# A two-layer encoder on one core: query tiles and later U tiles as one matmul of 512 columns and one of 256, with the halves added on DVE

## Chip, core and metric

The kernel runs on one core of one Trainium2 chip. The time is that of one execution on the device, in microseconds. The engines are TensorE (PE; PEld is its loading of weights), VectorE (DVE), ScalarE (ACT), GpSimd (POOL) and SyncE (SP), which only issues the loads of weights here.

## What is computed

256 tokens of width 1024 pass through two layers. Each has a token mixer (gated DeltaNet in layer 0, Mamba-2 SSD in layer 1) and then a PEER mixer, which retrieves experts by product keys. All is in float32. The change is in PEER:

```python
def _peer(h, w_q, sub_keys, u_tab, v_tab):
    q = (ht @ w_q).reshape(n_tok, PEER_HEADS, 2, PEER_HALF)
    s = jnp.einsum('thpd,hpkd->thpk', q, sub_keys).astype(jnp.float32)
    s_top, i_top = lax.top_k(s, PEER_TOPK)
    ...
    best, pos = lax.top_k(cand, PEER_TOPK)
    expert = jnp.take_along_axis(cand_id, pos, axis=-1)
    gate = jax.nn.softmax(best, axis=-1)
    ...
        act = jax.nn.gelu(jnp.einsum('thkd,td->thk', u_tab[eb], xb).astype(jnp.float32), approximate=False) * gb
        return jnp.einsum('thk,thkd->td', act.astype(v_tab.dtype), v_tab[eb])
```

There are 128 x 128 experts, 8 heads, two keys a head and the 16 best of each.

## The kernel before

**Split operands.** A float32 product is made of three faster ones. Each operand is split into a high part, rounded to the type fp32r, and a low part, the rest; the kernel computes high x high, high x low and low x high. `part_mm` issues the three matmuls. The tokens' parts are `hT[0]` and `hT[1]`, each 8 slices of 128 x 256 (slice k covers 128 of the 1024 channels). A weight tile of 128 x 1024 (512 KB) is loaded by SP into one of four places of `ring`. ScalarE copies it, half by half, into the high part (`split_half`), and POOL or DVE subtracts to get the low part (`rest_of_unit`). `w_part` has room for four halves, that is two tiles, so half s of tile n+2 can be converted once TensorE has used half s of tile n.

**The dense PEER.** The kernel doesn't gather experts. It goes through all 128 tiles of U (128 experts each) and computes the hidden value of every expert for every token: tile i gives 128 experts x 256 tokens in bank `PS[i % 2]` (`hidden`, which calls `columns`: 8 slices, 24 matmuls of 256 columns). Meanwhile it builds `p_map`, the gate of each expert for each token, mostly zeros. The weighted hidden values then multiply the 128 tiles of V (`values`). A PEER layer runs in these stages:

1. Query: 16 tiles of `peer_wq`, banks 4 and 5 in turn (`route` on TensorE). ScalarE copies each finished bank to `p_qT`. Then come the scores, and DVE's top-16 and gates, which take until about tile 56 of U.
2. Early U tiles, 0 to 55: ScalarE's Gelu writes straight into `p_map`.
3. Late rounds, tiles 56 to 119. In round q of these TensorE runs `hidden` of tile 57+q, then the map matmuls of four tokens (`maps4`). DVE runs `weigh_maps` (L1291: the last round's maps, out of their bank, times what stands in `p_map`), `one_hots` for the next round (L1281 and L1284) and `weigh_hidden` (L1299: the Gelu of tile 56+q times its row of the map). ScalarE runs `late` (L1645: the Gelu of tile 56+q into `p_act`, between the two halves of the high part of tile 58+q, L1376) and `weighed_rows` for the next round (L1666 and L1672). POOL makes both low halves of each tile (L1735).
4. Tiles 120 to 127, without maps.
5. Value stage: DVE splits each row of the map (`parts`, L1333 and L1334) and makes the low parts of the V tiles from the third on (L890); TensorE runs 12 matmuls of 512 columns a tile.

Every engine runs its own list in order, and the lists meet in counting semaphores: `lo_ready` and `half_used` for the halves of weights, `p_gelu` for a Gelu (TensorE waits for that of tile i-2 before it writes the bank again), `p_gated` for the product of a row, `p_mapps` for maps in their bank.

## Time and profile before

| | |
|---|---|
| median of 3 runs | 2286.61 us (2285.64 to 2288.24) |
| profiled execution | 2287.4 us |
| its span, first to last instruction | 2285.2 us |
| TensorE, mean granted clock | 0.974 |
| query stage, layer 0 | about 293 to 338 us |
| late rounds, layer 0 | about 508 to 746 us |
| value stage, layer 0 | from 783 us |

The profile is of one execution. An engine's busy time is that of its instructions from start to end, and matmuls overlap, so a busy TensorE says that it is never empty, not how fast it goes; the pace is read from the starts of neighbouring instructions. The clock is given as a share of 2.4 GHz. Layer 1 has the same PEER stages with nearly the same windows (late rounds from 1651 us).

### The profile page before, as it was taken

The page shows a single profiled execution, that of the slowest core. Times are in us where ns is not written, and L with a number is a line of the kernel's source. Part 1 is how long each engine was busy: PE and PEld are TensorE (multiplying, and loading weights), DVE is VectorE, ACT ScalarE, POOL GpSimd, SP SyncE. Part 2 cuts the span into 40 slices and gives each one's busy share as a digit, 9 for nine tenths or more (in the row PEclk, how much of TensorE's full clock was granted, in tenths as well). Part 3 has the DMA queues.
Part 4 walks back from the last instruction along what each step waited for, and adds up shares of the span by engine and source line. Part 5 has one row for each costly group of instructions (what it writes and reads, how often), then busy time and mean ns, then how long its engine had stood idle before and what let it go on. Part 6 is the DMA issues. An engine that isn't in the chain of part 4 may idle for free.

```text
span 2285.2 us, 46234 instructions
## 1 busy us (share of the span) xinstructions
PE 2172.6 (95%) x14320; PEld 1976.9 (87%) x14320; DVE 1547.2 (68%) x3465; ACT 1332.4 (58%) x2706; POOL 1112.2 (49%) x883
## 2 busy tenths in 40 slices
PE   7989799999999999999898878999999999999998
PEld 6969699999999988888797557999999999888886
DVE  4776319985666577777767882199856665777776
ACT  6744355577777544444565664555777775444444
POOL 6851378987666600000176566779876775000000
PEclk9989899999999999999999888999999999999999
DMA  5510254555444566665544114545544445666664
GB/s 166 167 56 1 65 166 148 172 168 154 140 138 138 171 193 193 192 194 191 174 139 127 58 65 132 170 148 169 173 149 141 141 138 165 194 193 193 193 193 147
DMA packets 93891, 343.72 MB, mean 150 GB/s; under 512 B 10688, under 2 KB 10752, under 8 KB 93168
## 3 DMA queue, kind: packets, MB, share of 16 engines
q1 hardware_dynamic: 92592, 338.21, 47.2%
q0 software_dynamic: 928, 4.10, 0.6%
q8 instruction: 47, 0.77, 0.1%
q10 hardware_dynamic: 288, 0.34, 0.0%
q14 instruction: 36, 0.29, 0.0%
HBM read 341.56 MB, written 1.05 MB: 150 GB/s over the span
## 4 chain that ended last, share of the span: by engine, by line
PE 77%; POOL 7%; DVE 7%; issue 5%; ACT 3%; DMA 0%; POOLq 0%; DVEq 0%; ACTq 0%
PE bank L358 75%; POOL w_lo L1735 7%; DVE arena L1155 2%; DVE arena L1143 1%; DVE w_lo L890 1%; ACT w_hi L1376 1%; PE bank L378 0%; PE bank L521 0%; DMA small<-in_ssd_d 0%; ACT arena L1402 0%; ACT arena L1376 0%; DVE arena L863 0%; DVE arena L967 0%; DVE arena L988 0%; DVE arena L1198 0%
## 5 line engine op out<-in xcount | busy, mean ns | idle before, releaser
L1735 POOL TENSOR_TENSOR w_lo<-ring,w_hi 128x512 fp32r<-128x512 f32 x744 | 994.9, 1351 | 684.6 <-ACT w_hi L1376 672.3
L1376 ACT ACTIVATE w_hi<-ring 128x512 fp32r<-128x512 f32 x1280 | 801.9, 628 | 520.6 <-PE bank L358 518.9
L358 PE MATMUL bank<-hT_hi,w_hi 128*128 128x256 f32 x2688 | 780.5, 290 | 8.3 <-POOL w_lo L1735 6.3
L358 PE MATMUL bank<-hT_lo,w_hi 128*128 128x256 f32 x2688 | 761.7, 283 | 0.0
L358 PE MATMUL bank<-hT_hi,w_lo 128*128 128x256 f32 x2688 | 761.6, 283 | 0.0
L358 PEld LDWEIGHTS bank<-hT_hi,w_hi 128*128 128x128 f32 x2688 | 516.6, 192 | 19.3 <-POOL w_lo L1735 18.8
L358 PEld LDWEIGHTS bank<-hT_lo,w_hi 128*128 128x128 f32 x2688 | 517.0, 192 | 0.0
L358 PEld LDWEIGHTS bank<-hT_hi,w_lo 128*128 128x128 f32 x2688 | 516.1, 192 | 0.0
L890 DVE TENSOR_TENSOR w_lo<-ring,w_hi 128x512 fp32r<-128x512 f32 x536 | 377.2, 704 | 172.8 <-ACT w_hi L1376 167.6
L358 PE MATMUL bank<-w_hi,p_ag_hi 128*128 128x512 f32 x1024 | 398.4, 389 | 0.0
L358 PE MATMUL bank<-w_lo,p_ag_hi 128*128 128x512 f32 x1024 | 398.4, 389 | 0.0
L358 PE MATMUL bank<-w_hi,p_ag_lo 128*128 128x512 f32 x1024 | 398.3, 389 | 0.0
L358 PEld LDWEIGHTS bank<-w_lo,p_ag_hi 128*128 128x128 f32 x1024 | 192.2, 188 | 40.1
L358 PEld LDWEIGHTS bank<-w_hi,p_ag_lo 128*128 128x128 f32 x1024 | 192.2, 188 | 39.9
L358 PEld LDWEIGHTS bank<-w_hi,p_ag_hi 128*128 128x128 f32 x1024 | 192.2, 188 | 39.6
L1291 DVE TENSOR_TENSOR arena<-bank,arena 128x512 f32 (+1 forms) x128 | 88.6, 692 | 166.6 <-PE bank L358 166.6
L358 PEld LDWEIGHTS bank<-arena 128*128 128x128 f32 x1072 | 136.1, 204 | 36.8 <-POOL arena L1811 13.2
L358 PE MATMUL bank<-arena 128*128 128x128 f32 (+2 forms) x1072 | 147.6, 294 | 17.6 <-POOL arena L1811 7.1
L908 DVE SCALAR_TENSOR_TENSOR arena<-bank,small,arena 128x254 f32<-128x254 f32 x192 | 92.6, 483 | 55.9 <-ACT arena L1376 50.7
L1672 ACT ACTIVATE work<-work,small 128x128 f32<-128x128 f32 x256 | 112.7, 488 | 20.2 <-ACT work L1666 19.6
L1334 DVE TENSOR_TENSOR p_ag_lo<-arena,p_ag_hi 128x256 fp32r<-128x256 f32 x256 | 111.0, 434 | 8.9
L1645 ACT ACTIVATE work<-bank 128x256 f32<-128x256 f32 x144 | 55.1, 383 | 84.0 <-PE bank L358 84.0
(236 smaller groups left out, 2329.6 us busy)
## 6 DMA issues: line engine op xcount, KB each, us to landing
ring<-in_peer_u SPq DMA_DIRECT2D x256, 512.0 KB, 3.5
ring<-in_peer_v SPq DMA_DIRECT2D x256, 512.0 KB, 3.5
ring<-in_peer_wq SPq DMA_DIRECT2D x32, 512.0 KB, 3.5
ring<-in_gdn_qkv SPq DMA_DIRECT2D x24, 512.0 KB, 3.5
ring<-in_ssd_xbc SPq DMA_DIRECT2D x24, 512.0 KB, 3.5
ring<-in_ssd_z SPq DMA_DIRECT2D x16, 512.0 KB, 3.5
ring<-in_ssd_out SPq DMA_DIRECT2D x16, 512.0 KB, 3.5
ring<-in_gdn_z SPq DMA_DIRECT2D x8, 512.0 KB, 3.5
```

Source lines behind the costliest of these rows:

```text
L358: return pe.matmul(o, w, r, start=first, stop=last)
L890: dve.tensor_tensor(w_part[1][:, s, :], ring[:, n % RING, hf * 512:(hf + 1) * 512], w_part[0][:, s, :].bitcast(F32), ALU.subtract).then_in ...
L908: ins = dve.scalar_tensor_tensor(o, bank[:, lo + s:hi + s], taps[:, m, j:j + 1], o, ALU.mult, ALU.add)
L1143: last = dve.tensor_scalar(s_E[:, h % 2, st, d, :], PS[h % 2][:, d * T + st * P:d * T + (st + 1) * P], s_ac[:, st, d * SH + h:d * SH + h + ...
L1155: last = dve.scalar_tensor_tensor(s_M[:, h % 2, st, d, :], s_CB[:, g, st, d, :], s_dt[:, st, d * SH + h:d * SH + h + 1], s_E[:, h % 2, st, ...
L1291: dve.tensor_tensor(v, PS[2 + q % 4][:, :].rearrange("p (t i) -> p i t", t=4), v, ALU.mult).then_inc(SEM["p_mul"], 1)
L1334: dve.tensor_tensor(p_ag[1][:, i % 2, :], v, p_ag[0][:, i % 2, :].bitcast(F32), ALU.subtract).then_inc(SEM["p_ag"], 1)
L1376: return act.activation(o, i, ACT.Copy, scale=scale)
L1645: act.activation(p_act[:, i % 2, :], PS[i % 2][:, 0:T], ACT.Gelu).then_inc(SEM["p_gelu"], 1)
L1672: act.activation(row, row, ACT.Relu, bias=p_T[:, 2, tok], scale=p_minus[:, tok]).then_inc(SEM["p_hotS"], 1)
L1735: pool.tensor_tensor(w_part[1][:, s, :], ring[:, n % RING, hf * 512:(hf + 1) * 512], w_part[0][:, s, :].bitcast(F32), ALU.subtract).then_i ...
```

## The change

The two parts of the tokens now lie in one tensor, `hT_both`, so that one matmul can stream both. `columns_wide` does for a tile what `columns` does: with the high weights loaded it streams 512 columns, the 256 high and the 256 low ones, into the two halves of a bank, and with the low weights it adds 256 high columns to the second half. Each tile's bank now holds two halves whose sum is the result. It is used for the query tiles and for U tiles 56 to 127. The early U tiles keep `columns`.

DVE adds the halves with a `tensor_reduce`: in the query stage straight into `p_qT` (ScalarE's copy goes away), in the late rounds into a new tile `p_raw` (`add_halves`), from which ScalarE's Gelu reads. So ScalarE waits for a new semaphore, `p_halves`, instead of for TensorE's `half_used`. On DVE `add_halves` of a tile stands last in the round, and `weigh_hidden` is of the tile before. The last 8 rows are weighed ahead of the first two `parts` of the value stage; before, they stood behind them. Loads and other matmuls don't change.

```diff
@@ -145,7 +145,8 @@
         x_sb = sb("x_sb", [P, NT, D])
 
 
-        hT = [sb("hT_" + s, [P, KD, T], F32R) for s in ("hi", "lo")]
+        hT_both = sb("hT", [P, 2, KD, T], F32R)
+        hT = [hT_both[:, p, :, :] for p in range(2)]
         ring = sb("ring", [P, RING, D])
         w_part = [sb("w_" + s, [P, SPLIT, D // 2], F32R) for s in ("hi", "lo")]
         p_ag = [sb("p_ag_" + s, [P, 2, T], F32R) for s in ("hi", "lo")]
@@ -282,6 +283,7 @@
 
 
         row = [flat(p[0:SH, :, :], "s t") for p in p_ag]
+        p_raw = sb("p_raw", [P, T])[:, :]
         pick = sb("pick", [SH, SH], F32R)[:, :]
 
 
@@ -404,6 +406,18 @@
                         await_h(fresh, k)
                         last = part_mm(o, lambda p: w_part[p][:, s, kk * P:(kk + 1) * P],
                                        lambda p: hT[p][:, k, :], k == 0, k == KD - 1)
+                    last.then_inc(half_used, 1)
+
+            def columns_wide(bank, n, it=0, step=0, fresh=None):
+
+                for hf in range(2):
+                    s = half(n, hf, it, step)
+                    for kk in range(KD // 2):
+                        k = KD // 2 * hf + kk
+                        await_h(fresh, k)
+                        c = slice(kk * P, (kk + 1) * P)
+                        mm(bank[:, :].rearrange("p (e t) -> p e t", e=2), w_part[0][:, s, c], hT_both[:, :, k, :], k == 0, False)
+                        last = mm(bank[:, T:2 * T], w_part[1][:, s, c], hT[0][:, k, :], False, k == KD - 1)
                     last.then_inc(half_used, 1)
 
             def rows_of(n, src, first, last_one, it=0, step=0):
@@ -728,7 +742,7 @@
                     if m >= 2:
                         pe.wait_ge(SEM["p_q"], HP * lyr + m - 1)
 
-                    by_channel(("pq", lyr, m), 4 + m % 2, None if m else 2 * lyr + 1)
+                    columns_wide(PS[4 + m % 2], at[("pq", lyr, m)], fresh=None if m else 2 * lyr + 1)
                 pe.wait_ge(SEM["p_q"], HP * (lyr + 1))
                 pe.wait_ge(keys_loaded, 16 * (lyr + 1))
                 for g in range(8):
@@ -745,7 +759,10 @@
                 if tiles or i >= 2:
 
                     pe.wait_ge(SEM["p_gelu"], it * tiles + (P * lyr + i - 1))
-                columns(PS[i % 2][:, 0:T], n, it, 8)
+                if i < EARLY:
+                    columns(PS[i % 2][:, 0:T], n, it, 8)
+                else:
+                    columns_wide(PS[i % 2], n, it, 8)
 
             def values(lyr, i, n, it=0, tiles=0, first=False, last_one=False):
                 pe.wait_ge(SEM["p_ag"], it * tiles + (P * lyr + i + 1))
@@ -1215,6 +1232,9 @@
                 return all_four(lambda v, top, idx: dve.max_index(idx[:, 8:16], top[:, 8:16], v))
 
             def route(lyr):
+                for m in range(HP):
+                    dve.wait_ge(half_used, 2 * (at[("pq", lyr, m)] + 1))
+                    dve.tensor_reduce(p_qT[:, m, :], PS[4 + m % 2][:, :].rearrange("p (e t) -> p t e", e=2), AX.X, ALU.add).then_inc(SEM["p_q"], 1)
                 for g in range(8):
                     t, first_head = g // 2 % 2, 8 * (g // 4) + 4 * (g % 2)
                     dve.wait_ge(SEM["p_s"], 8 * lyr + g + 1)
@@ -1299,16 +1319,24 @@
                     dve.tensor_tensor(row, p_act[:, i % 2, :], row, ALU.mult).then_inc(SEM["p_gated"], 1)
                     dve.wait_ge(SEM["p_gated"], it * 4 + ((P - EARLY) * lyr + i - EARLY + 1))
 
+                def add_halves(i, it=0):
+
+                    dve.wait_ge(half_used, it * 8 + 2 * (tables[lyr] + i + 1))
+                    if not isinstance(it, int) or i > EARLY:
+                        dve.wait_ge(SEM["p_gelu"], it * 4 + (P * lyr + i))
+                    b = PS[i % 2]
+                    dve.tensor_reduce(p_raw, b[:, :].rearrange("p (e t) -> p t e", e=2), AX.X, ALU.add).then_inc(SEM["p_halves"], 1)
+
                 def maps_and_hidden(it, first=False, last=False):
                     for q in range(4):
+                        i, loop = (EARLY + 4 * it + q, 0) if isinstance(it, int) else (EARLY + q, it)
                         if not first or q:
                             weigh_maps(it, q - 1)
                         if not last or q < 3:
                             one_hots(it, q + 1, first)
-                        if isinstance(it, int):
-                            weigh_hidden(EARLY + 4 * it + q)
-                        else:
-                            weigh_hidden(EARLY + q, it)
+                        if not first or q:
+                            weigh_hidden(i - 1, loop)
+                        add_halves(i, loop)
 
                 one_hots(0, 0, True)
                 maps_and_hidden(0, True)
@@ -1316,6 +1344,10 @@
                     maps_and_hidden(it)
                 maps_and_hidden(T // 16 - 1, last=True)
                 weigh_maps(T // 16, -1)
+                for i in range(EARLY + T // 4, P):
+                    add_halves(i)
+                    weigh_hidden(i - 1)
+                weigh_hidden(P - 1)
 
             def experts(lyr):
                 n0 = tables[lyr]
@@ -1337,9 +1369,6 @@
                 dve.wait_ge(SEM["p_mul"], 64 * (lyr + 1))
                 parts(0)
                 parts(1)
-                for i in range(EARLY + T // 4, P):
-                    dve.wait_ge(SEM["p_gelu"], P * lyr + i + 1)
-                    dve.tensor_tensor(p_map[:, i, :], p_act[:, i % 2, :], p_map[:, i, :], ALU.mult).then_inc(SEM["p_gated"], 1)
                 dve.wait_ge(SEM["p_gated"], (P - EARLY) * (lyr + 1))
                 dve.wait_ge(lo_ready, 2 * (n1 + 2))
                 with dve.Fori(0, P // 4 - 1) as it:
@@ -1614,10 +1643,7 @@
 
             def route(lyr):
                 for m in range(HP):
-                    split_half(at[("pq", lyr, m)] + 2, 0)
-                    act.wait_ge(half_used, 2 * (at[("pq", lyr, m)] + 1))
-                    copy(p_qT[:, m, :], PS[4 + m % 2][:, 0:T]).then_inc(SEM["p_q"], 1)
-                    split_half(at[("pq", lyr, m)] + 2, 1)
+                    split(at[("pq", lyr, m)] + 2)
                 for g in range(8):
                     t, first_head = g // 2 % 2, 8 * (g // 4) + 4 * (g % 2)
                     act.wait_ge(SEM["p_sps"], 8 * lyr + g + 1)
@@ -1638,11 +1664,11 @@
                 def late(i, it=0):
 
                     split_half(n0 + i + 2, 0, it, 8)
-                    act.wait_ge(half_used, it * 8 + 2 * (n0 + i + 1))
+                    act.wait_ge(SEM["p_halves"], it * 4 + ((P - EARLY) * lyr + i - EARLY + 1))
                     if not isinstance(it, int) or i >= EARLY + 2:
 
                         act.wait_ge(SEM["p_gated"], it * 4 + ((P - EARLY) * lyr + i - EARLY - 1))
-                    act.activation(p_act[:, i % 2, :], PS[i % 2][:, 0:T], ACT.Gelu).then_inc(SEM["p_gelu"], 1)
+                    act.activation(p_act[:, i % 2, :], p_raw, ACT.Gelu).then_inc(SEM["p_gelu"], 1)
                     split_half(n0 + i + 2, 1, it, 8)
 
                 for i in range(4):
```

## Rows read from the trace of the kernel before

**Rows 1.** The page, section 1: busy time and share of the span.

```profile
PE 2172.6 (95%) x14320; PEld 1976.9 (87%) x14320; DVE 1547.2 (68%) x3465; ACT 1332.4 (58%) x2706; POOL 1112.2 (49%) x883
```

**Rows 2.** Windows of layer 0: busy us of PE, PEld, DVE, ACT, POOL; clock.

```profile
293.00:337.70 44.70, 44.70 (x370) 44.70 (x370) 1.71 (x5) 23.82 (x47) 36.97 (x29) 0.99 0.55 167
427.00:464.00 37.00, 36.13 (x278) 33.70 (x277) 36.90 (x29) 21.18 (x38) 35.07 (x23) 1.00 0.53 164
508.00:746.00 238.00, 238.00 (x2022) 238.00 (x2021) 141.96 (x300) 190.41 (x441) 169.76 (x130) 1.00 0.46 144
...
800.00:900.00 100.00, 100.00 (x443) 82.81 (x442) 74.33 (x148) 46.35 (x74) 0.00 (x0) 1.00 0.64 193
```

**Rows 3.** The chain of waits over the late rounds, 508 to 746 us.

```profile
507.96 238.07 PE bank L358 x2020
```

**Rows 4.** Timeline of TensorE, one late round.

```profile
563.08 0.36 PE L358 MATMUL bank<-hT_hi,w_hi 128*128 128x256 f32 x1
563.28 0.28 PE L358 MATMUL bank<-hT_lo,w_hi 128*128 128x256 f32 x1
563.40 0.28 PE L358 MATMUL bank<-hT_hi,w_lo 128*128 128x256 f32 x1
...
566.84 0.36 PE L358 MATMUL bank<-hT_hi,w_hi 128*128 128x256 f32 x1
```

**Rows 5.** Timeline of DVE, a late round and one four later.

```profile
563.51 0.69 DVE L1291 TENSOR_TENSOR arena<-bank,arena 128x512 f32 x1 [1.26 <-PE bank L358]
564.36 0.69 DVE L1281 TENSOR_TENSOR p_ag_hi<-bank,work 128x512 fp32r<-128x512 f32 x1
...
565.60 0.42 DVE L1299 TENSOR_TENSOR arena<-work,arena 128x256 f32 x1
...
578.58 0.69 DVE L1291 TENSOR_TENSOR arena<-bank,arena 128x512 f32 x1 [1.26 <-PE bank L358]
```

**Rows 6.** Timeline of ScalarE, the same round.

```profile
562.55 0.38 ACT L1645 ACTIVATE work<-bank 128x256 f32<-128x256 f32 x1 [0.58 <-PE bank L358]
562.83 0.62 ACT L1376 ACTIVATE w_hi<-ring 128x512 fp32r<-128x512 f32 x1
...
564.34 0.88 ACT L1672 ACTIVATE work<-work,small 128x128 f32<-128x128 f32 x2 [0.17 <-ACT work L1666]
565.12 0.62 ACT L1376 ACTIVATE w_hi<-ring 128x512 fp32r<-128x512 f32 x1
...
566.61 0.62 ACT L1376 ACTIVATE w_hi<-ring 128x512 fp32r<-128x512 f32 x1
```

**Rows 7.** Timeline of POOL, the next round.

```profile
567.31 1.29 POOL L1735 TENSOR_TENSOR w_lo<-ring,w_hi 128x512 fp32r<-128x512 f32 x1 [0.15 <-ACT w_hi L1376]
```

**Rows 8.** DVE's tensor_reduce, by line: duration ns min/median/max.

```profile
L1258 DVE TENSOR_REDUCE arena<-arena x32: 673/676/686, 450.7 to 1628.4; 128x32 f32<-128x512 f32 x32
```

**Rows 9.** Timeline in gated DeltaNet: ScalarE released by DVE.

```profile
147.94 0.42 DVE L979 TENSOR_TENSOR arena<-arena 128x256 f32<-128x256 f32 x1
...
148.40 0.42 ACT L1494 ACTIVATE arena<-arena 128x256 f32<-128x256 f32 x1 [1.60 <-DVE arena L979]
```

**Rows 10.** Timeline, early tiles beside the top-16: TensorE released by POOL.

```profile
436.43 3.44 POOL L1735 TENSOR_TENSOR w_lo<-ring,w_hi 128x512 fp32r<-128x512 f32 x2
...
439.92 0.19 PEld L358 LDWEIGHTS bank<-hT_hi,w_hi 128*128 128x128 f32 x1 [0.21 <-POOL w_lo L1735]
...
440.15 0.28 PE L358 MATMUL bank<-hT_lo,w_hi 128*128 128x256 f32 x1
```

**Rows 11.** Timelines of TensorE, ScalarE and DVE where the value stage begins.

```profile
782.94 0.40 PE L358 MATMUL bank<-w_hi,p_ag_hi 128*128 128x512 f32 x1
...
783.14 0.39 ACT L1645 ACTIVATE work<-bank 128x256 f32<-128x256 f32 x1 [0.75 <-PE bank L358]
...
787.16 0.28 DVE L1333 CAST p_ag_hi<-arena 128x256 fp32r x1
787.48 0.42 DVE L1334 TENSOR_TENSOR p_ag_lo<-arena,p_ag_hi 128x256 fp32r<-128x256 f32 x1
```

More of the change, by code:

```diff
@@ L306, in hybrid_encoder @@
             "s_cbps s_cb s_bc s_d s_e s_off s_m s_yps s_y s_ss s_mean s_root "
-            "p_q p_sps p_s p_ex p_exd p_key p_Tps p_Tsb p_hot p_hotS p_hotB p_dist p_mapps p_mul p_gelu p_gated p_ag_hi p_ag "
+            "p_q p_sps p_s p_ex p_exd p_key p_Tps p_Tsb p_hot p_hotS p_hotB p_dist p_halves p_mapps p_mul p_gelu p_gated p_ag_hi p_ag "
             "finished stored").split()}
```

## The prediction

> **What bounds the kernel now.** I read the page first: TensorE is busy 95% of the span and no other engine above 68% [rows 1]. A share over the span doesn't say what ends a stage, so I took windows of one layer. In the query stage, in the late rounds and in the value stage TensorE is busy in all of each window at a granted clock of 0.99 to 1.00, its upper level of 2.4 GHz [rows 2]. The chain of waits over the late rounds is one unbroken piece of matmuls, 238 us long [rows 3]. So in the stages that the change touches the pace is TensorE's, and time is gained by shortening its queue, as long as nobody else then becomes late. That needs the timeline of each engine over one round. The reader is to see in it that a late round takes 3.77 us (15.07 us for four) [rows 5], that DVE works 2.51 us of it and then waits for TensorE, and that ScalarE's Gelu starts 0.53 us before TensorE opens the next tile at 563.08 [rows 4, 6].
>
> Matmuls of 256 columns follow each other at 0.120 us [rows 4], those of 512 at 0.226 us (100 us for 443) [rows 2]. A U tile of 24 matmuls takes 2.88 us, which leaves 0.89 us of a late round for its map matmuls.
>
> **The change, part by part: TensorE.** For each of a tile's 8 slices of the contraction three matmuls of 256 columns (0.360 us) become one of 512 and one of 256 (0.346 us): 0.014 us less a slice, 0.11 us a tile. The columns streamed are the same, and only one matmul's fixed part goes. The tile falls to 2.77 us, a half of it to 1.38 us, the late round to 3.66 us. Touched are 16 query tiles and 72 late U tiles in each of two layers, 1408 slices: 19.7 us if nothing else moved. What the 256-column matmul costs directly behind one of 512 no row shows. Its columns alone bound it at 0.107 us (256 at 2.4 GHz) from below and 0.120 us is its row; I take the row, since the 512-column stream also runs 0.013 us over its columns.
>
> The rows show 0.013 us over the column time at both sizes. The Trainium skill (TensorE: Matmul & The Clock Gate, Back-to-back issue gap) gives N/2.4 + 2.5 ns, so three matmuls would take 328 ns and two 325 ns, and all 1408 slices would give back 3.5 us instead of 19.7 us. I go by the rows.
>
> **ScalarE and DVE in the query stage.** The copy of the finished bank (0.38 us) goes from ScalarE to DVE, as a reduce over the two halves. DVE is busy 1.71 us in this stage [rows 2] and takes it within the 2.77 us of the next tile. The nearest row for it reads 512 elements a partition and takes 0.676 us [rows 8]; DVE's other work on 512 columns of a bank takes 0.69 us [rows 5], and I take 0.69 us. POOL needs 1.27 us a half, 2.55 us a tile (36.97 us for 29) [rows 2], under 2.77 us. So the stage gains 32 x 0.11 = 3.5 us. Only the last bank of each layer is seen in full, because the scores wait for it: 0.69 - 0.38 = 0.3 us, 0.6 us in all. Net -2.9 us.
>
> **The late rounds.** Here the Gelu of tile i no longer waits for TensorE alone. It waits for DVE's sum, and DVE issues that sum last in its round: behind the map product, the one-hots and the product of the tile before (weigh_maps, one_hots, weigh_hidden). The first of these waits for maps that TensorE runs after tile i. Behind the Gelu on ScalarE stands the second half of tile i+2's high part, behind that POOL's low part, and TensorE needs both in the middle of tile i+2. I lay this out from T, TensorE's first U matmul after the maps (563.08) [rows 4]:
>
> - the map product starts 0.43 us after T, and the tile product ends 2.51 us later (563.51 to 566.02) [rows 5];
> - 0.16 us for DVE to see its own signal, as between the first two rows of its round [rows 5]; then the sum, 0.69 us;
> - 0.04 us to ScalarE [rows 9], 0.28 us from the start of the Gelu to that of the high part, 0.62 us for it [rows 6];
> - 0.08 us to POOL (567.23 to 567.31), 1.29 us for the low part [rows 7], 0.05 us to TensorE (439.87 to 439.92), and 0.11 us because a matmul after a wait is followed at 0.23 us instead of 0.12 us [rows 10].
>
> That is 6.26 us after T. TensorE is then in the round after the next T, and has half a tile (1.38 us) and the maps (0.89 us) left before the following one. Two rounds take 6.26 + 1.38 + 0.89 = 8.53 us, one takes 4.27 us, where TensorE alone would need 3.66 us and takes 3.77 us now. So TensorE stands about 0.6 us in each tile, and a round is 0.50 us longer. In the kernel before the same ring has ample room: the Gelu starts before T, the second high part ends 0.37 us after it, and POOL is done long before TensorE comes there.
>
> The other waits fit inside 4.27 us. ScalarE's rows for the next maps end at T + 6.5 (Gelu start at 3.83, 2.67 us from there to the end of its row at 564.34) [rows 6] and are wanted at T + 7.6. The first half of tile i+3 is ready at T + 8.5, when TensorE comes for it, and a little lateness there is hidden by the stall in the middle. The bank is released at T + 4.3, which is hidden in the same way. DVE ends its round at T + 3.8 and is idle until the next maps. SP's loads are for tiles further on.
>
> There are 64 such rounds a layer. I take 63, one to close the ring: 126 x 0.50 = +63 us. The 7 tiles after them have no maps. There DVE is free when the tile ends, and the low part comes about 3.3 us after it, before the 4.15 us (a tile and a half) at which it is wanted. They gain 14 x 0.11 = 1.6 us.
>
> **The start of the value stage.** Now TensorE goes from the last U tile to the first V tile at once (782.94), and the last Gelu follows 0.20 us later [rows 11], since DVE had already split the first two rows of the map. In the changed kernel both splits stand behind the last product. So TensorE waits for: 0.20 us, the sum 0.69, 0.04, the Gelu 0.38, 0.04, the product 0.42 [rows 5], 0.16, the cast and the rest 0.28 + 0.04 + 0.42 [rows 11], 0.05. That is 2.7 us a layer, +5.4 us. The two V tiles that follow (12 x 0.226 = 2.7 us each) cover DVE's start on the third.
>
> **The sum.** +63 - 1.6 + 5.4 - 2.9 = +63.9 us on the profiled execution's 2287.4 us, 2351.3 us. The median of the runs is 0.8 us lower: 2350.5 us.
>
> **Bounds.** Chain, short: the 512-column successor at 0.107 us (-0.05 us in a half) and all four handoffs and the restart at nothing (-0.44 us) give 8.04 us for two rounds, 4.02 us each, +32 us. Chain, long: POOL's half beside a busy DVE took 1.72 us (3.44 us for two) [rows 10] instead of 1.29 us, and DVE will be busier; two rounds of 8.96 us, 4.48 us each, +27 us on the forecast, 2378 us.
>
> **Rivals.** *The ring stays open.* The second half of tile i+2 is ready in time and TensorE keeps the pace: -19.7 + 5.4 + 0.6 = -13.7 us, 2273 us, faster. For it speaks that ScalarE and POOL have idle time in each round now. It decides if the low part comes by T + 5.05 (2 x 3.66 - 1.38 - 0.89), 1.2 us earlier than my sum; the queue order leaves no step out. Chance 0.10. *Only the bank binds.* The halves come in time, but tile i+2 can't start before Gelu i has ended (T + 4.26): two rounds of 4.26 + 0.11 + 2.77 + 0.89 = 8.03 us, 4.01 us each, 126 x 0.24 + 0.9 = +31 us, 2318 us. Chance 0.08. *POOL or the sum is slower than its row*, as in the long bound, 2378 us: 0.15. *The clock falls.* With TensorE standing one part in seven, and 2.7 us once a layer, its clock could drop to 1.2 GHz for stretches. A tile's 6144 columns then take 5.12 us, a round with doubled maps 6.9 us, and 20 such rounds bring 2403 us. Against it: with a wait in each half tile, beside the top-16, it kept 1.00 [rows 2]. Chance 0.03. *The parts cancel* within the bound below: 0.02. The forecast itself: 0.62.
>
> **How the numbers follow.** The range of 2317 to 2380 us runs from the bank's case to the long bound and leaves out the open ring and the clock. A measurement of this kernel can tell about 0.2%, 4.6 us, from no change. Faster holds the open ring and a little more, 0.11; the same 0.03; slower 0.86.
>
> **What the profile after would show.** Late rounds 4.2 to 4.4 us apart at DVE's map product, with TensorE stopped once in the middle of a tile, by POOL; Gelu starting some 3.8 us after T instead of before it; 0.346 us for each pair of matmuls; query tiles 2.77 us apart; a gap of about 2.7 us before the first V matmul. Rounds of 3.66 us would refute the ring, rounds of 4.0 us with the stop at a tile's start would show the bank, and a POOL half or a DVE sum much over 1.3 or 0.7 us the long case.

## The result, and the profile after

The kernel became slower: 2402.2 us median of 4 runs (2394.25 to 2405.38) against 2286.97 us (2285.64 to 2288.24), a ratio of 1.0499 (95% interval 1.0486 to 1.0512). The forecast was 2350.5 us with a range of 2317 to 2380 us. The direction was right and the size was not: the loss is 115 us, 1.8 times the 64 us forecast.

The profiled execution of after took 2394.25 us, the shortest of its four; its span is 2392.4 us. The two spans, cut at DVE's map products and at TensorE's matmuls, show where the 107.3 us between them went:

| stretch, us | before | after | difference |
|---|---|---|---|
| start to the first late map product, layer 0 | 525.76 | 521.16 | -4.60 |
| 63 late rounds, layer 0 | 237.30 | 288.21 | +50.91 |
| last map product to the last U matmul | 19.76 | 19.19 | -0.57 |
| from there to the first late map product, layer 1 | 886.43 | 889.98 | +3.55 |
| 63 late rounds, layer 1 | 237.30 | 289.21 | +51.91 |
| last map product to the last U matmul | 19.76 | 19.19 | -0.57 |
| from there to the end | 358.86 | 365.50 | +6.64 |

The first and the fourth stretch also hold mixers, where the clock differs between executions (the last section has it). So nearly all of it lies in the late rounds, 102.8 us in both layers: a round takes 4.58 us instead of 3.77 us. The page, section 1, answers to [rows 1]:

```profile
PE 2189.7 (92%) x12912; PEld 1902.8 (80%) x12912; DVE 1717.2 (72%) x3641; ACT 1317.2 (55%) x2674; POOL 1109.6 (46%) x883
```

DVE is up by 170 us, of which the 144 sums of the late tiles are 100 us. TensorE is still "busy" 92%, and nothing on the line tells of a loss of 5%. The windows do. These are the query stage, late rounds, and the value stage later on (against [rows 2]):

```profile
293.00:337.70 44.70, 43.92 (x260) 38.72 (x259) 11.31 (x18) 20.27 (x32) 41.20 (x32) 1.00 0.54 177
520.00:760.00 240.00, 206.76 (x1259) 176.19 (x1258) 180.20 (x312) 152.11 (x364) 133.70 (x105) 1.00 0.36 113
...
900.00:1000.00 100.00, 100.00 (x443) 82.81 (x442) 73.85 (x147) 46.55 (x74) 0.00 (x0) 1.00 0.61 194
```

In the late rounds TensorE is empty for 33 us of 240 at the full clock, and the chain of waits over 520 to 740 us, which was one piece of matmuls before [rows 3], has none of them in it:

```profile
by line: POOL w_lo L1761 49.6%; issue 49.6%; POOLq L1759 1.2%; POOLq L1771 0.4%
```

The timelines of one pair of rounds say why, TensorE first (against [rows 4]), with the weight load that waited in the middle of the tile:

```profile
566.00 0.47 PE L360 MATMUL bank<-hT,w_hi 128*128 128x512 f32 x1
...
568.86 1.05 PE L360 MATMUL bank<-work,p_ag_lo 128*128 128x128 f32 x8
571.05 0.49 PE L360 MATMUL bank<-hT,w_hi 128*128 128x512 f32 x1 [1.13 <-ACT work L1671]
...
572.86 0.19 PEld L360 LDWEIGHTS bank<-hT,w_hi 128*128 128x128 f32 x1 [0.47 <-POOL w_lo L1761]
...
574.39 1.05 PE L360 MATMUL bank<-work,p_ag_hi 128*128 128x128 f32 x8
575.19 0.47 PE L360 MATMUL bank<-hT,w_hi 128*128 128x512 f32 x1
```

Then DVE, ScalarE and POOL in the same round (against [rows 5 to 7]):

```profile
566.37 0.69 DVE L1311 TENSOR_TENSOR arena<-bank,arena 128x512 f32 x1 [1.59 <-PE bank L360]
567.22 0.69 DVE L1301 TENSOR_TENSOR p_ag_hi<-bank,work 128x512 fp32r<-128x512 f32 x1
567.82 0.72 DVE L1304 TENSOR_SCALAR work<-bank,work 128x128 f32<-128x128 f32 x2
568.46 1.12 DVE L1319 TENSOR_TENSOR arena<-work,arena 128x256 f32 x1
569.77 0.69 DVE L1328 TENSOR_REDUCE p_raw<-bank 128x256 f32<-128x512 f32 x1 [0.19 <-DVE arena L1319]
```

```profile
570.50 0.42 ACT L1671 ACTIVATE work<-p_raw 128x256 f32<-128x256 f32 x1 [2.57 <-DVE p_raw L1328]
570.82 0.62 ACT L1405 ACTIVATE w_hi<-ring 128x512 fp32r<-128x512 f32 x1
```

```profile
568.01 1.29 POOL L1761 TENSOR_TENSOR w_lo<-ring,w_hi 128x512 fp32r<-128x512 f32 x1 [0.88 <-ACT w_hi L1405]
571.51 1.29 POOL L1761 TENSOR_TENSOR w_lo<-ring,w_hi 128x512 fp32r<-128x512 f32 x1 [2.22 <-ACT w_hi L1405]
```

From T = 566.00 to the next such point, 575.19, are 9.19 us for two rounds (the mean of the layer is 9.15 us). This is the forecast's ring, link by link: map product, one-hots, the product of a row (L1319), the sum, the Gelu, the second high half, POOL's low half, TensorE at 572.86, half a tile and the maps. One link has another size. The product of the row was put at 0.42 us and took 1.12 us. It starts at 568.46 and ends at 569.58; POOL's half runs from 568.01 to 569.30. Of the 63 products of layer 0's late rounds 59 start while POOL is at a half, and each of these ends 0.28 to 0.29 us after that half. The sum takes its forecast 0.69 us and POOL its 1.29 us. Over all rounds (durations min/median/max by source line):

```profile
L1319 DVE TENSOR_TENSOR arena<-work,arena x144: 415/723/1537, 523.1 to 2029.5; 128x256 f32 x112, 128x256 f32<-128x256 f32 x32
...
L1328 DVE TENSOR_REDUCE p_raw<-bank x144: 691/692/693, 517.5 to 2027.3; 128x256 f32<-128x512 f32 x144
```

Where the value stage begins (against [rows 11]), TensorE's last U matmul starts at 828.56 and the first V matmul at 833.37, 4.81 us later, where before there were 0.12 us:

```profile
828.56 0.28 PE L360 MATMUL bank<-hT,w_lo 128*128 128x256 f32 x1
833.37 0.51 PE L360 MATMUL bank<-w_hi,p_ag_hi 128*128 128x512 f32 x1 [4.53 <-issue]
...
834.10 0.63 PE L360 MATMUL bank<-w_hi,p_ag_lo 128*128 128x512 f32 x1
834.53 0.63 PE L360 MATMUL bank<-w_hi,p_ag_hi 128*128 128x512 f32 x1
```

```profile
829.54 2.94 DVE L1319 TENSOR_TENSOR arena<-work,arena 128x256 f32<-128x256 f32 x2
```

```profile
834.00:838.00 4.00, 4.00 (x12) 3.06 (x12) 0.69 (x1) 0.65 (x2) 0.00 (x0) 0.62 0.49 175
838.00:842.00 4.00, 4.00 (x19) 3.32 (x18) 2.65 (x6) 1.88 (x3) 0.00 (x0) 1.00 0.38 99
```

Two products take 2.94 us there beside POOL's last three halves, and eight V matmuls then follow the one before at 0.43 us instead of 0.23 us: the granted clock of 834 to 838 us is 0.62, mostly the lower level, 1.2 GHz. In the 50 us from the last U matmul on, 192 V matmuls start, where before 220 did; 28 x 0.227 us = 6.4 us a layer, and the last line of the table has 6.64 us.

### The profile page after: what moved, and what is told of

Its sections match the earlier page's. It is cut to its first block, busy times and chain, and to the rows that moved or that the text cites. A ratio compares the mean times of both kernels' runs of the same rounds, so it can differ in the third digit from the quotient of the medians.

```text
span 2392.4 us, 43818 instructions
## 1 busy us (share of the span) xinstructions
PE 2189.7 (92%) x12912; PEld 1902.8 (80%) x12912; DVE 1717.2 (72%) x3641; ACT 1317.2 (55%) x2674; POOL 1109.6 (46%) x883
## 3 DMA queue, kind: packets, MB, share of 16 engines
HBM read 341.56 MB, written 1.05 MB: 143 GB/s over the span
## 4 chain that ended last, share of the span: by engine, by line
PE 49%; POOL 21%; issue 20%; DVE 7%; ACT 3%; POOLq 1%; DMA 1%; DVEq 0%; ACTq 0%
PE bank L360 48%; POOL w_lo L1761 21%; DVE arena L1172 2%; DVE arena L1160 1%; DVE w_lo L907 1%; PE bank L535 1%; ACT w_hi L1405 0%; PE bank L380 0%; DMA small<-in_ssd_d 0%; POOLq L1759 0%; ACT arena L1405 0%; ACT arena L1431 0%; DVE arena L880 0%; DVE arena L984 0%; DVE arena L1005 0%
## 5 line engine op out<-in xcount | busy, mean ns | idle before, releaser
L360 PE MATMUL bank<-hT,w_hi 128*128 128x256 f32 (+1 forms) x3968 | 993.5, 330 | 88.1 <-ACT work L1671 70.1
L360 PEld LDWEIGHTS bank<-hT,w_hi 128*128 128x128 f32 x3968 | 665.0, 191 | 183.8 <-issue 81.5
L360 PE MATMUL bank<-hT,w_lo 128*128 128x256 f32 x2688 | 756.7, 282 | 0.0
L360 PEld LDWEIGHTS bank<-hT,w_lo 128*128 128x128 f32 x2688 | 512.8, 191 | 0.0
L1671 ACT ACTIVATE work<-p_raw 128x256 f32<-128x256 f32 x144 | 60.4, 419 | 211.7 <-DVE p_raw L1328 211.7
L360 PE MATMUL bank<-w_hi,hT 128*128 128x512 f32 x384 | 135.9, 417 | 13.5 <-ACT arena L1598 10.0
L1328 DVE TENSOR_REDUCE p_raw<-bank 128x256 f32<-128x512 f32 x144 | 99.6, 692 | 66.9 <-PE bank L360 44.6
L1319 DVE TENSOR_TENSOR arena<-work,arena 128x256 f32 (+1 forms) x144 | 123.7, 859 | 0.1
```

Of the source, the lines that this page charges most:

```text
L360: return pe.matmul(o, w, r, start=first, stop=last)
L1319: dve.tensor_tensor(row, p_act[:, i % 2, :], row, ALU.mult).then_inc(SEM["p_gated"], 1)
L1328: dve.tensor_reduce(p_raw, b[:, :].rearrange("p (e t) -> p t e", e=2), AX.X, ALU.add).then_inc(SEM["p_halves"], 1)
L1671: act.activation(p_act[:, i % 2, :], p_raw, ACT.Gelu).then_inc(SEM["p_gelu"], 1)
```

## Experiments

All ratios are against the kernel before on the same chip. "Rounds" are the mean distance of the 64 late map products of layer 0. The theory after the result was: the ring holds, and what made it longer is the product of a row, held up by POOL when both read SBUF. The rivals: the ring is longer for some other wait; the wide matmuls are slow themselves; the clock.

**The query stage alone.** U tiles and the order of DVE as before.

> Only the query tiles use the 512-column matmul and DVE's sum; the U tiles, their Gelu and the order of DVE's late rounds are those of the kernel before. My theory, by which the added time all comes from the late rounds and the start of the value stage: 32 tiles at 2.77 us instead of 2.88 us, less 0.6 us for the longer last copies, so 2.9 us less than before, about 2284 us. Rival, that part of the loss comes from DVE working beside POOL already in the query stage: slower than before, 2290 us or more.

Measured: 2282.33 us (11 runs), ratio 0.9982 (0.9973 to 0.9991), -4.0 us. The query tiles of after stand 2.77 us apart (`hT,w_hi` at 293.10, 295.87, 298.64). This part gains what was forecast, -2.9 us, or a little more.

**The wide matmuls without the sum.** Query and U tiles 56 to 127 as in after, but nobody adds the halves: ScalarE reads the first half of the bank as before, so the low weights' and low tokens' share is left out.

> All matmuls of the change, but nothing adds the halves: ScalarE reads the first half of the bank, in the query stage and for each Gelu, as it read the bank before, and DVE's rounds are those of before. The part of each product that lies in the second half (low tokens and low weights) is left out of the result. It prices the matmuls alone. By the rows of before (0.120 and 0.226 us) 1408 slices give back 0.014 us each: 19.7 us less than before, 2267 us, late rounds of 3.66 us. By N/2.4 + 2.5 ns of the Trainium skill only 3.5 us less, 2283.5 us. Rival to both, that a 256-column matmul behind a 512-column one costs more than 0.120 us: no gain, 2287 us.

Measured: 2269.97 us (2268.0 to 2273.69), ratio 0.9933 (0.9918 to 0.9948), -16.4 us. Rounds are 3.684 us, 0.08 us less than before where 0.11 us had been forecast, and the chain over 560 to 740 us is matmuls alone again. TensorE's timeline:

```profile
600.53 0.39 PE L360 MATMUL bank<-hT,w_hi 128*128 128x512 f32 x1
600.76 0.27 PE L360 MATMUL bank<-hT,w_lo 128*128 128x256 f32 x1
600.87 0.40 PE L360 MATMUL bank<-hT,w_hi 128*128 128x512 f32 x1
```

A pair takes 0.345 us (four take 1.38 us from 599.84 to 601.22), as forecast. The matmuls do save some 16 us, so the loss comes with the sum, its place and the order behind it. The formula of the Trainium skill (TensorE: Matmul & The Clock Gate, Back-to-back issue gap), which the page gives for an isolated matmul and by which 3.5 us would have come back, does not hold for these streams: the pair's 345 ns are 25 ns over the 320 ns of its 768 columns at 2.4 GHz, 12.5 ns for each matmul and not 2.5.

**The Gelu's output in PSUM.** In the late rounds ScalarE writes it to a free bank, so `weigh_hidden` reads one operand from PSUM and one from SBUF. Nothing else moves.

```diff
+        def acted(i, rounds=True):
+            return PS[6][:, (i % 2) * T:(i % 2 + 1) * T] if rounds else p_act[:, i % 2, :]
...
-                    act.activation(p_act[:, i % 2, :], p_raw, ACT.Gelu).then_inc(SEM["p_gelu"], 1)
+                    act.activation(acted(i, not isinstance(it, int) or i < EARLY + T // 4), p_raw, ACT.Gelu).then_inc(SEM["p_gelu"], 1)
```

> The changed kernel, with one thing different: in the late rounds the Gelu writes to PSUM bank 6 instead of to SBUF, so that DVE's product of the hidden row (0.42 us in the kernel before, 0.90 us on average in the changed one) has only one operand in SBUF. My theory now: the ring through DVE, ScalarE and POOL sets the round, and it is 0.7 us longer in two rounds than I added up because this product and POOL's low half, both with two operands in SBUF, slow DVE down when they meet. Then the product falls to about 0.42 us, two rounds take 8.5 us instead of 9.2 us, and the time falls by 126 x 0.34 = 43 us to about 2359 us. Rival, that the product is long because DVE is waiting inside it for something else or that the ring is not what binds: product or round unchanged, 2400 us.

Measured: 2355.09 us (2354.26 to 2360.85), ratio 1.0299 (1.0283 to 1.0315). Groups of instructions over 560 to 740 us, first of after, then of this kernel:

```profile
L1319 DVE TENSOR_TENSOR arena<-work,arena 128x256 f32 x40 | 35.1, 877 | 0.0
```

```profile
L1322 DVE TENSOR_TENSOR arena<-bank,arena 128x256 f32 x42 | 17.4, 413 | 0.0
```

The product is back at 0.413 us every time, POOL working as before beside it. Rounds are 4.235 us, where the ring with a product of 0.42 us had been forecast at 4.27 us. This is the experiment that settles the mis-sized term: 47 us of the loss hang on where one operand lies. TensorE still waits at the start of every second tile, for the Gelu that frees the bank, and again in its middle for POOL:

```profile
641.57 0.49 PE L363 MATMUL bank<-hT,w_hi 128*128 128x512 f32 x1 [0.42 <-ACT bank L1674]
```

**The sum first in its round,** ahead of the map product, instead of last.

```diff
                     for q in range(4):
+                        add_halves(i, loop)
                         if not first or q:
                             weigh_maps(it, q - 1)
...
                             weigh_hidden(i - 1, loop)
-                        add_halves(i, loop)
```

> The changed kernel with DVE's sum of the halves first in its round, ahead of the map product, the one-hots and the product of the row before, instead of last. All work is the same. My theory: the loss comes from the sum's place in DVE's queue, which closes a ring of two rounds. With the sum first the Gelu follows the tile's end by about 1 us, the low part is ready 3.3 us after the tile, over a microsecond early, and the ring is open. The round is then the larger of TensorE's 3.66 us and DVE's own work (3.2 us, waits of 0.3 us, and up to 0.8 us where it meets POOL): 3.7 to 4.0 us, so 2275 to 2320 us. Rival, that it is the amount of DVE's work (one more pass over a bank a tile) or its meeting with POOL that costs, wherever it stands: 4.4 us a round or more, 2370 us or more.

Measured: 2286.76 us (2281.65 to 2287.57, 10 runs), ratio 0.9997 (0.9987 to 1.0006). Rounds are 3.686 us, and the chain is one piece again:

```profile
559.91 180.30 PE bank L360 x1174
```

The ring is open, though DVE has the same work. The value stage still starts 4.8 us late, and with the clock that gives the gain of the matmuls back. The product was mostly short here, 0.50 us in the mean, for it starts when POOL's half is nearly over, in this round at 603.45 where the half ends at 603.53 (DVE, then POOL):

```profile
603.45 0.41 DVE L1319 TENSOR_TENSOR arena<-work,arena 128x256 f32 x1
```

```profile
600.86 2.67 POOL L1761 TENSOR_TENSOR w_lo<-ring,w_hi 128x512 fp32r<-128x512 f32 x2 [0.86 <-ACT w_hi L1405]
604.39 1.29 POOL L1761 TENSOR_TENSOR w_lo<-ring,w_hi 128x512 fp32r<-128x512 f32 x1 [0.87 <-ACT w_hi L1405]
```

**The sum third,** behind the one-hots and ahead of the product: the same line, moved up by one call.

> The changed kernel with DVE's sum one place earlier: behind the map product and the one-hots, ahead of the product of the row before. Theory of the ring: in the changed kernel the sum starts 3.77 us after T (TensorE's first U matmul after the maps) and two rounds take 9.20 us. Here it should start 2.5 us after T, two rounds fall by 1.25 us to 7.95 us, a round is 3.98 us, and the time falls by 126 x 0.62 = 78 us to about 2324 us. Rival, that the loss lies in the amount of DVE's work and not in the sum's place: rounds stay above 4.4 us, 2380 us or more.

Measured: 2325.08 us (2322.92 to 2326.8), ratio 1.0165 (1.0149 to 1.018); rounds 4.015 us, where the ring said 3.98 us. The product still meets POOL (0.871 us in the mean), but it is no link of the ring any more: over 560 to 740 us what a map product waits for is always TensorE's maps, never the product in front of it.

```profile
L1311 DVE TENSOR_TENSOR arena<-bank,arena 128x512 f32 x45 | 31.1, 692 | 21.6 <-PE bank L360 21.6
```

**The sum second,** between the map product and the one-hots.

> The changed kernel with the sum directly behind the map product. Theory of the ring: the sum starts about 1.2 us after T, so by the same count two rounds would take 6.6 us, which is below TensorE's own 7.4 us: the ring is open and nothing is left of its price. The round is TensorE's 3.69 us as with the sum first, and the time equals that of the kernel with the sum first, 2287 us, since the start of the value stage is the same in both. Rival, that each place earlier gives its share: faster than with the sum first or rounds clearly above 3.7 us.

Measured: 2327.43 us (2326.22 to 2329.21), ratio 1.0173 (1.0157 to 1.0189), a miss by 40 us; rounds 4.025 us. The trace shows a link that my ring didn't have: the next round's map product waits for the product in front of it, and that is held by POOL (the same group over 560 to 740 us, then DVE, then POOL):

```profile
L1311 DVE TENSOR_TENSOR arena<-bank,arena 128x512 f32 x45 | 31.1, 692 | 16.3 <-PE bank L360 7.8 <-DVE arena L1319 5.6
```

```profile
611.88 1.46 DVE L1319 TENSOR_TENSOR arena<-work,arena 128x256 f32 x1
613.47 0.69 DVE L1311 TENSOR_TENSOR arena<-bank,arena 128x512 f32 x1
```

```profile
611.78 1.28 POOL L1761 TENSOR_TENSOR w_lo<-ring,w_hi 128x512 fp32r<-128x512 f32 x1 [0.36 <-ACT w_hi L1405]
```

**The sum second and the Gelu's output in PSUM** tests that reading: the place stays, the meeting costs nothing. The product also waits for the Gelu of its own tile, so that DVE and ScalarE don't touch the bank at once.

> The sum directly behind the map product, as in the run that came out at 2327 us instead of 2287 us, and besides the Gelu of the late rounds writes to PSUM bank 6; the product of the row before waits for the Gelu of its own tile too, which has ended by then, so that the two engines don't touch the bank at once. Theory: the sum's place is early enough there, and the rounds of 4.03 us come from the product, which meets POOL's low half (0.94 us on average, up to 1.5 us) and so fills DVE's queue. With one operand in PSUM it takes 0.41 us, DVE's round 3.3 us, TensorE sets the pace again: 3.69 us a round, about 2287 us. Rival, that the sum's place or its bank costs there: rounds stay near 4.0 us and the time near 2327 us.

Measured: 2284.85 us (2281.59 to 2287.38, 10 runs), ratio 0.9989 (0.998 to 0.9999); rounds 3.685 us. So the second place is early enough, and the 43 us more of the kernel without PSUM were the product's alone.

**A copy in the sum's place, and no wide matmul in the U tiles.** U tiles run three matmuls of 256 columns as before, and DVE copies the bank to `p_raw` last in its round. The query stage stays as in after.

> The late rounds in the changed order, but with the three matmuls of 256 columns of the kernel before: DVE, last in its round, only copies the finished half bank (256 columns) for the Gelu; the query tiles are as changed. It asks whether the loss needs the 512-column matmul at all. Theory of the ring: the copy takes about 0.4 us instead of 0.69 us (-0.3 us in two rounds), TensorE's half tile 1.44 us instead of 1.38 us (+0.06 us): two rounds of about 8.95 us, 4.48 us a round, so about 2387 us. Rival, that the wide matmul itself costs in the late rounds (its banks or its waits): near the kernel before, 2290 to 2330 us.

Measured: 2373.52 us (2371.03 to 2376.07), ratio 1.038 (1.0364 to 1.0396); rounds 4.355 us, the copy 0.424 us, the product 0.727 us in the mean. The loss is there without any wide U matmul: it is the step through DVE, last in its round. The 13.5 us under the expectation fit a product that was held less in the rounds that the ring goes through: 1.05 and 0.82 us in turn, where after has about 1.20 and 1.13 us. That is 0.23 us less in two rounds, 63 x 0.23 = 14.5 us.

**The splits ahead of the last eight sums.** `parts(0)` and `parts(1)` stand before the tail tiles' sums and products, as they did before the change. Once with the sum first in its round, once in the order of after, once in that order with the Gelu's output in PSUM.

```diff
...
-                for i in range(EARLY + T // 4, P):
-                    add_halves(i)
-                    weigh_hidden(i - 1)
-                weigh_hidden(P - 1)
+                tail[:] = [add_halves, weigh_hidden]
...
                 parts(0)
                 parts(1)
+                for i in range(EARLY + T // 4, P):
+                    tail[0](i)
+                    tail[1](i - 1)
+                tail[1](P - 1)
```

> The sum first in DVE's round, and besides DVE splits the first two rows of the map ahead of the last eight sums and products, as in the kernel before. It prices the start of the value stage: with the sum first TensorE stands 4.8 us there in each layer and then runs its first 11 or 12 matmuls of the V tiles at 0.43 us instead of 0.23 us, together 7.2 us a layer. Theory: both go, 14.5 us less than with the sum first, about 2272 us, which is faster than the kernel before by 0.6%. Rival, that the wait there only moves to the third V tile, which DVE splits later: no change, 2287 us.

> The changed kernel with only the order at the start of the value stage restored: DVE splits the first two rows of the map ahead of the last eight sums and products. In the changed kernel TensorE stands 4.8 us there in each layer and issues 192 V matmuls in the 50 us behind the last U matmul, against 220 in the kernel before: 28 x 0.227 = 6.4 us a layer. Theory: about 12.7 us less than the changed kernel, 2389 us. Rival, that the wait moves to the third V tile: 2402 us.

> The changed kernel with both: the Gelu of the late rounds to PSUM bank 6 and the first two rows of the map split early. What is left is the ring alone, without the meeting of DVE and POOL and without the wait at the value stage. Theory: the parts add up, 2355 us less 12.7 us, about 2342 us; my forecast's own steps (ring at 4.27 us a round, -2.9 us in the query stage, no wait at the value stage) give 2345 us. Rival, that the two share a cause: 2350 us or more.

Measured: 2273.83 us (2270.74 to 2275.49), ratio 0.9939 (0.9926 to 0.9953); 2393.81 us (2391.19 to 2396.59), ratio 1.0462 (1.0445 to 1.0479); 2353.33 us (2343.91 to 2356.33), ratio 1.0281 (1.0254 to 1.0308). In all three the first V matmul follows the last U matmul within 0.12 us, at once at the pace of the full clock, and 217 or 218 V matmuls start in 50 us. So the start of the value stage is worth nearly what was read: in the second kernel 26 V matmuls more than in after, 5.9 us a layer. But something comes back. From the last map product to the last U matmul the second kernel takes 21.64 us, after 19.19 us; the third 21.73 us and the first 20.57 us. A split is held by POOL too (DVE, then POOL, of the second):

```profile
811.89 1.11 DVE L1364 CAST p_ag_hi<-arena 128x256 fp32r<-128x256 f32 x1
813.03 0.43 DVE L1365 TENSOR_TENSOR p_ag_lo<-arena,p_ag_hi 128x256 fp32r<-128x256 f32 x1
```

```profile
810.31 2.53 POOL L1764 TENSOR_TENSOR w_lo<-ring,w_hi 128x512 fp32r<-128x512 f32 x2 [0.21 <-ACT w_hi L1408]
```

The sum of tile 120 starts only at 814.04, and TensorE stands for its Gelu. The net is -5.9 + 2.45 = -3.45 us a layer, -6.9 us in all, and 2393.81 is 8.4 us under 2402.2. The third misses its expectation of 2342 us by 11 us. 5 us are this tail. By stage it does what the second does against the kernel with the splits behind: the last stretch, from the last U matmul of layer 1 on, falls from 365.74 to 359.63 us, the tail grows by 2.56 us. But its median is only 1.8 us lower, and its four executions range over 12 us (2343.91 to 2356.33). The rest I lay to the spread between executions, told of below; that was argued, not shown.

**The splits between the tail tiles,** `parts(0)` after the product of tile 122 and `parts(1)` after that of 123, with the sum first.

> The sum stands first in its round, and the two splits of the map's rows stand between the products of tiles 122 and 124 of the tail, neither ahead of all tail tiles (as in the kernel with the splits early, 2273.8 us) nor behind them (2286.8 us). My account: the splits ahead of the tail make the sum of tile 120 late, and TensorE stands 1.4 us a layer (20.57 us from the last map product to the last U matmul, where 19.17 us is the figure with the splits behind). In the tail DVE is idle 1.75 us a tile, one split needs 0.7 us, and even if it is held by POOL's half for 1.2 us it fits. So the tail falls back to 19.2 us, the value stage still starts 0.12 us after the last U matmul, and the time is 2273.8 - 2.8 = 2271 us. Rival: a split held by POOL's half pushes the next sum past its slack, so the tail stays near 20.5 us: 2274 us or more.

Measured: 2274.59 us (2269.78 to 2275.88), ratio 0.9943 (0.9929 to 0.9956). The rival was right, by the trace: the tail is 20.71 us in layer 0 and 19.93 us in layer 1, not 19.2 us. The time alone, 3.6 us above the forecast in a spread of 6 us, could hardly tell. The product, the cast and the subtraction each wait for one of POOL's halves, which stand back to back there:

```profile
764.45 1.56 DVE L1321 TENSOR_TENSOR arena<-work,arena 128x256 f32<-128x256 f32 x1
766.04 1.27 DVE L1364 CAST p_ag_hi<-arena 128x256 fp32r<-128x256 f32 x1
767.34 1.39 DVE L1365 TENSOR_TENSOR p_ag_lo<-arena,p_ag_hi 128x256 fp32r<-128x256 f32 x1
768.65 0.68 DVE L1330 TENSOR_REDUCE p_raw<-bank 128x256 f32<-128x512 f32 x1
```

```profile
759.06 9.38 POOL L1764 TENSOR_TENSOR w_lo<-ring,w_hi 128x512 fp32r<-128x512 f32 x7
```

The fastest kernels of the study that compute the whole result have the sum first and the splits ahead of the tail or within it: 12 to 13 us, 0.6%, faster than before. The edit was a good one with its sum in another place.

## Why the prediction was right in kind and wrong in size

- **What bounds the kernel** (right). TensorE's queue set the pace, and shortening it with the rest untouched gave 16.4 us of the 19.7 us forecast; the rounds gained 0.08 us each instead of 0.11 us.
- **TensorE, a pair at 0.346 us** (right): 0.345 us.
- **The query stage, -2.9 us** (right): -4.0 us by itself, with an interval that holds -2.9.
- **The late rounds, +63 us** (the ring was right, its size wrong). Its order, its links and the two rounds that it closes over are what the trace shows, and with the product at 0.413 us the rounds are 4.235 us against 4.27. The step that failed is the first term of the list, "the tile product ends 2.51 us later (563.51 to 566.02) [rows 5]". It took 0.42 us for the product from a kernel in which it starts in POOL's pause, at 565.60, 0.22 us ahead of POOL's next half, and in which that half is the longer one (from 565.82, 1.33 us instead of 1.29 us). In after it took 1.12 us in the round laid out, because POOL was already at a half. Two rounds grew from 8.53 to 9.19 us, 0.33 us a round, and 126 x 0.33 = +42 us. Over both layers the rounds cost 102.8 us, 39.8 us more than the 63 us forecast.
- **The long bound of 2378 us** named the right meeting and let the wrong side pay. It took POOL's 1.72 us beside a busy DVE [rows 10]. In after POOL kept 1.29 us and the sum 0.69 us, and DVE's product waited. No bound priced that.
- **Where TensorE stops** (half right). One tile in two is stopped, in its middle by POOL, but it waits at its start as well, by 1.13 us for the Gelu that frees the bank. "The bank is released at T + 4.3, which is hidden" did not hold, not even with the short product, where TensorE waits 0.42 us for it (641.57 in the kernel with the Gelu's output in PSUM). It costs nothing of its own: POOL's low half, which TensorE waits for next, comes later.
- **The tail, -1.6 us**: -0.57 us a layer, -1.1 us.
- **The value stage's start, +5.4 us** (right in kind, too small): 6.4 us a layer, 12.8 us in all. The gap was put at 2.7 us and was 4.8 us, since two products took 2.94 us in POOL's company; and some 1.6 us more went to V matmuls at 1.2 GHz. The clock had been priced for the rounds only.
- **The sum**: 2350.5 + 42 + 7.4 = 2400 us, against 2402.2 us measured. That it comes so near is in part luck, since the executions of after spread over 11 us.
- **The rivals.** The open ring, the bank alone and the cancelling parts did not come. In the rounds the clock stayed at 1.00.

## What to carry to other kernels

A row's duration belongs to what ran beside it: before an operation is moved in its queue, look at which other engine's row it will lie beside and which of the two starts first, and price it by a row where they overlap in that order. A result that a long ring waits for goes first in its engine's round; here moving one call, with DVE's work the same, was worth 115 us. Where an engine must meet POOL, give its operation one PSUM operand, or start it in POOL's pause.

## What the runs showed of the hardware

**DVE beside POOL.** A DVE product with both operands in SBUF that starts while POOL subtracts from SBUF to SBUF ends 0.28 us after POOL's half ends: 569.58 after 569.30, and 613.34 after 613.06. Alone it takes 0.42 us. POOL keeps 1.28 to 1.31 us there. The other way round POOL is held. In the kernel before, the product of [rows 5] starts first, at 565.60, and POOL's half beside it takes 1.33 us. With the sum second, a product and a half that start within 0.02 us of each other take 0.41 and 1.57 us:

```profile
565.82 1.33 POOL L1735 TENSOR_TENSOR w_lo<-ring,w_hi 128x512 fp32r<-128x512 f32 x1 [0.99 <-ACT w_hi L1376]
```

```profile
604.77 0.41 DVE L1319 TENSOR_TENSOR arena<-work,arena 128x256 f32 x1
```

```profile
604.75 1.57 POOL L1761 TENSOR_TENSOR w_lo<-ring,w_hi 128x512 fp32r<-128x512 f32 x1 [1.39 <-ACT w_hi L1405]
```

With one operand in PSUM the product takes 0.413 us beside the same POOL work, and so the sum and the map product keep 0.69 us. The cast of a map row, with a single SBUF operand, is held as well (1.11 and 1.27 us for 0.29 to 0.30 us). The Trainium skill (SBUF — State Buffer, Who interferes with whom) says so: a DVE instruction with two SBUF inputs takes its second one through a read port that it shares with GpSimd, the lock is exclusive and the order of issue decides who waits, a reduce never meets it, and casts can. The traces agree: the product takes 0.42 us against up to 1.56 us, the cast 0.29 us against 1.1 to 1.3 us, and the top-16's reduces from SBUF, all beside POOL's halves, keep 0.67 to 0.69 us [rows 8].

**A pause and the clock.** After 4.1 to 4.8 us without a matmul, in the kernels with the splits behind, the granted clock was down to the lower level for a while: 7 to 13 V matmuls at 0.43 us instead of 0.23 us. In the late rounds stops of up to 1.3 us, one in every two rounds, left it at 1.00.

**The spread between executions.** The executions of after spread over 11 us, and the granted clock went with it: 0.976 over the whole in that of 2394.25 us, 0.972 in that of 2399.41 us, 0.969 and 0.970 in those of 2404.99 and 2405.38 us. In the token mixer of layer 1, which no edit touches, the same 118 matmuls took 25.0 us at a clock of 0.93 in the profiled execution of after and 29.7 us at 0.76 in that of the kernel with its splits early:

```profile
1348.80:1373.80 25.00, 24.95 (x118) 17.66 (x118) 21.68 (x57) 13.83 (x33) 14.85 (x19) 0.93 0.20 65
```

```profile
1347.00:1376.70 29.70, 29.69 (x117) 21.11 (x118) 23.18 (x57) 14.02 (x33) 14.75 (x19) 0.76 0.16 54
```

So differences of a few us between single executions of this kernel can come from the mixers alone, and are to be read by stage.
